# The output projection's x traffic moves to SyncE, and its first chunk starts inside the memory attention

## The reference, cut to what matters

```python
mixed = jnp.concatenate([out_a, out_b, out_m], axis=-1)   # 1024 x 2048
return x + mixed @ w_o                                    # w_o is 2048 x 2048
```

## Time and profile before

| | us |
|---|---|
| median of 3 runs | 1513.98 (1510.68 to 1514.11) |
| profiled execution, its own time | 1507.98 |
| its span in the profile | 1506.2 |
| PE busy, of the span | 1464.1 (97%) |
| DVE, ACT busy | 671.9, 469.2 |

### The profile page before, as it was taken

The page is one execution under the profiler, slowest core; times in us unless marked ns, Lnnn a source line. Parts: engine busy times, 40 slices in busy tenths (PEclk is TensorE's granted clock), DMA queues, the critical chain, the costliest instruction groups (busy, mean ns, idle before and its releaser), DMA issues.

```text
span 1506.2 us, 17987 instructions
## 1 busy us (share of the span) xinstructions
PE 1464.1 (97%) x7118; PEld 1195.7 (79%) x7118; DVE 671.9 (45%) x1055; ACT 469.2 (31%) x842; POOL 130.6 (9%) x141
## 2 busy tenths in 40 slices
PE   9999999999999999999999998889998999999997
PEld 7888888888888888887887787656777788888886
DVE  4332241442614131312226767975659654444542
ACT  4551301313131020201234456974456411111110
POOL 1010000202001000000001022100000011111110
PEclk9999999999999999999999999999999999999999
DMA  9541231121123121221444521540020233333331
GB/s 359 196 107 56 98 111 55 42 101 52 42 102 108 57 97 56 81 72 43 167 154 155 181 84 42 155 127 15 15 71 17 75 112 106 105 112 105 108 109 49
DMA packets 48812, 146.78 MB, mean 97 GB/s; under 512 B 5616, under 2 KB 9712, under 8 KB 47472
## 3 DMA queue, kind: packets, MB, share of 16 engines
q1 hardware_dynamic: 33136, 84.42, 17.8%
q0 software_dynamic: 15472, 61.51, 11.7%
q10 hardware_dynamic: 144, 0.02, 0.0%
HBM read 117.61 MB, written 28.32 MB: 97 GB/s over the span
## 4 chain that ended last, share of the span: by engine, by line
PE 90%; ACT 5%; DVE 3%; issue 1%; DMA 0%; POOL 0%; ACTq 0%; SPq 0%; DVEq 0%
PE ps L1537 26%; PE ps L1539 26%; PE ps L1538 26%; ACT a_p L805 3%; PE ps L1756 2%; PE ps L1719 2%; PE ps L1720 2%; PE ps L1737 1%; PE ps L1723 1%; PE ps L1762 1%; PE ps L1591 0%; PE ps L1590 0%; DVE w_lo L938 0%; ACT st L803 0%; PE ps L1741 0%
## 5 line engine op out<-in xcount | busy, mean ns | idle before, releaser
L938 DVE TENSOR_TENSOR w_lo<-w_raw,w_hi 128x1024 fp32r<-128x1024 f32 x87 | 106.6, 1225 | 504.0 <-ACT w_hi L608 503.6
L608 ACT ACTIVATE w_hi<-w_raw 128x1024 fp32r<-128x1024 f32 x89 | 94.2, 1059 | 593.8 <-PE ps L1539 573.9
L1537 PE MATMUL ps<-w_hi,h_hi 128*128 128x512 f32 x640 | 249.5, 390 | 1.4 <-DVE h_lo L953 1.4
L1539 PE MATMUL ps<-w_hi,h_lo 128*128 128x512 f32 x640 | 249.4, 390 | 0.0
L1538 PE MATMUL ps<-w_lo,h_hi 128*128 128x512 f32 x640 | 249.3, 390 | 0.0
L1539 PE MATMUL ps<-h_hi,w_lo 128*128 128x512 f32 x512 | 199.5, 390 | 0.0
L1537 PE MATMUL ps<-h_hi,w_hi 128*128 128x512 f32 x512 | 199.5, 390 | 0.0
L1538 PE MATMUL ps<-h_lo,w_hi 128*128 128x512 f32 x512 | 199.5, 390 | 0.0
L1538 PE MATMUL ps<-mixed_lo,z_hi 128*128 128x512 f32 x384 | 149.6, 390 | 0.0
L1537 PEld LDWEIGHTS ps<-w_hi,h_hi 128*128 128x128 f32 x640 | 120.2, 188 | 26.5 <-issue 1.6
L1539 PEld LDWEIGHTS ps<-w_hi,h_lo 128*128 128x128 f32 x640 | 120.2, 188 | 24.9
(11 more groups left out here) (270 smaller groups left out, 2090.9 us busy)
## 6 DMA issues: line engine op xcount, KB each, us to landing
w_raw<-in_w SPq DMA_DIRECT2D x89, 512.0 KB, 3.5
z<-in_w_out SPq DMA_DIRECT2D x64, 256.0 KB, 2.7
x_nat<-in_x POOLq DMA_DIRECT2D x8, 1024.0 KB, 8.6
mixed<-gate_s POOLq DMA_DIRECT2D x16, 512.0 KB, 4.9
xq<-in_xT POOLq DMA_DIRECT2D x32, 256.0 KB, 4.5
out_y<-xq POOLq DMA_DIRECT2D x32, 256.0 KB, 2.6
x_raw<-in_xT SPq DMA_DIRECT2D x7, 1024.0 KB, 18.2
gate_s<-T POOLq DMA_DIRECT2D x3, 2048.0 KB, 7.0
```

What stands on the lines that cost most here:

```text
L608: a.activation(w_hi[:, n % SPLIT, :], w_raw[:, n % RAW, :], ACT.Copy).then_inc(hi_ready, 1)
L938: v.tensor_tensor(w_lo[:, n % SPLIT, :], w_raw[:, n % RAW, :], w_hi[:, n % SPLIT, :].bitcast(F32), ALU.subtract).then_inc(lo_ready, 1)
L1537: mm(out, a_hi, b_hi, start=start, stop=False)
L1539: return mm(out, a_lo, b_hi, start=False, stop=stop)
```

## The change

- The order of the units in a visit becomes 0, 1, 4, 2, 5, 3, 6, 7 (`ORDER`, `unit(c)`), in the loads of z and on all engines; the weights are read from the same array at the other index.
- The x loads and the stores of the result go from POOL's queue to SP's, between the loads of z.
- PE does chunk 0's products P1, P5, P7, P2, P3 inside or just after the last steps of the memory attention, P4 behind the last value product, and P6 behind the last gate.
- Preparation is redistributed, in `ahead` and in the first chunks of the projection, and three buffers change place.

```diff
+ORDER = (0, 1, 4, 2, 5, 3, 6, 7)
@@ sync (SP)
-                sp.dma_start(z[c % ZRING][:, 0:4, :], io["w_out"][c]).then_inc(z_loaded[c % ZRING], 16)
+                sp.dma_start(z[c % ZRING][:, 0:4, :], io["w_out"][c // NUNIT * NUNIT + unit(c)]).then_inc(z_loaded[c % ZRING], 16)
+            def load_xq(visit):
+                for q in range(4):
+                    wait(sp, xq_moved[q], 32 * visit)
+                    sp.dma_start(xq[:, q, :], quad(io["xT"], visit, q)).then_inc(xq_moved[q], 16)
+            def store_y(visit):
+                for q in range(4):
+                    sp.wait_ge(drained, 9 * visit + 6 + q)
+                    sp.dma_start(quad(io["yT"], visit, q), xq[:, q, :]).then_inc(xq_moved[q], 16)
             for c in range(2, NOUT):
                 load_z(c)
+                if c == 2:
+                    load_xq(0)
+                if c >= NUNIT and c % NUNIT == 3:
+                    store_y(c // NUNIT - 1)
+                if c >= NUNIT and c % NUNIT == 4:
+                    load_xq(c // NUNIT)
+            store_y(NVISIT - 1)
@@ gpsimd (POOL): its loads of x and stores of the result are removed
@@ scalar (ACT)
             def ahead(c):
-                if 2 <= c <= 5:
-                    left_high(1 + (c - 2) // 2, c % 2)
-                if c == 6:
-                    z_high(0)
+                if c in (2, 3):
+                    left_high(1, c - 2)
+                if c == 5:
+                    act.wait_ge(B.pv, len(BSTEPS))
+                if c in (4, 5):
+                    z_high(c - 4)
+                if c in (6, 7):
+                    left_high(2, c - 6)
+                    plain_high(c + 2)
...
-            act.wait_ge(M.gated, TT)
+            act.wait_ge(M.pv, TT)
             for c in range(NOUT):
-                if c + 1 < NOUT:
+                if 2 <= c + 1 < NOUT:
                     z_high(c + 1)
-                if c == 0:
+                if c in (1, 3, 4):
+                    k = {1: 10, 3: 12, 4: 14}[c]
+                    plain_high(k)
+                    plain_high(k + 1)
+                if c == 2:
                     left_high(3, 0)
                     left_high(3, 1)
-                elif c < 5:
-                    for k in (2 * c + 6, 2 * c + 7):
-                        plain_high(k)
-                if u == NBLOCK:
+                if c % NUNIT == 6:
@@ vector (DVE)
             def ahead(c):
-                if c < 4:
-                    left_sums(1 + c // 2, c % 2)
-                elif c < 6:
-                    left_low(1, c - 4)
-                    if c == 5:
-                        z_make(0)
-                else:
-                    left_low(2, c - 6)
+                if c in (0, 1):
+                    left_sums(1, c)
+                if c in (2, 3):
+                    z_make(c - 2)
+                if c in (5, 6):
+                    z_low(c - 5)
+                if c in (4, 5):
+                    left_sums(2, c - 4)
+                if c in (6, 7):
+                    left_low(1, c - 6)
...
-            z_low(0)
             gate(M, TT - 1, 1, TT // 2 - 1)
-            z_make(1)
             for c in range(NOUT):
-                if c + 1 < NOUT:
+                if 2 <= c + 1 < NOUT:
                     z_low(c + 1)
-                if c == 0:
+                if c == 2:
                     left_sums(3, 0)
                     left_sums(3, 1)
-                elif c < 3:
-                    left_low(3, c - 1)
-                if 2 <= c <= 6:
-                    for k in ((8,), (9, 10), (11, 12), (13, 14), (15,))[c - 2]:
-                        plain_low(k)
-                if u == (6 if visit == 0 else 4):
+                if c in (0, 2, 4, 5):
+                    k = {0: 8, 2: 10, 4: 12, 5: 14}[c]
+                    plain_low(k)
+                    plain_low(k + 1)
+                if c in (1, 3):
+                    left_low(2 + c // 2, 0)
+                    left_low(2 + c // 2, 1)
+                if u == 6:
                     partial_sums(visit)
-                if u == (7 if visit == 0 else 5):
+                if u == 7:
                     add_sums(visit)
@@ tensor (PE), in the memory attention's step body
+                        if beside and c == n - 1:
+                            beside(1)
...
                             value(at_, c - 1, 1 - par, i if par else i - 1)
+                        if beside and c == n - 2:
+                            beside(0)
                         turn_p(at_, c, par)
@@ tensor (PE)
+            def out_begun(part):
+                if part == 0:
+                    pe.wait_ge(z_lo_made, 1)
+                    pe.wait_ge(left_lo_made, 2)
+                    pe.wait_ge(M.qT, TT)
+                    product(0, P1)
+                elif part == 1:
+                    pe.wait_ge(M.exp, TT)
+                    product(0, P5)
+                    product(0, P7)
+                else:
+                    product(0, P2)
+                    product(0, P3)
...
+            out_begun(2)
+            value(M, TT - 1, 1, TT // 2 - 1)
-            pe.wait_ge(M.gated, TT)
             for c in range(NOUT):
...
+                if c == 0:
+                    product(0, P4)
+                    pe.wait_ge(M.gated, TT)
+                    ins = product(0, P6)
```

More of the change, by code:

```diff
@@ L266, in layer @@
         left_slo = [at(f"left_slo{u}", [P, 3, HALF], F32R, left_at[u] + 14336) for u in range(NBLOCK)]
-        plain_at = [RT + 8192, RT + 12288] + [RS + 4096 * k for k in range(6)]
+        plain_at = [RT + 12288, RS, small_at + 3584, RS + 4096, RS + 8192, RS + 12288, RT, RT + 4096]
         plain_hi = [at(f"plain_hi{k}", [P, SEQ], F32R, plain_at[k]) for k in range(KT - 2 * NBLOCK)]
@@ L271, in layer @@
         z_lo = [at(f"z_lo{i}", [P, 7, P], F32R, z_at[i]) for i in range(ZRING)]
-        zh_at = (R0 + 61440, small_at + 3584)
+        zh_at = (R0 + 61440, RT + 8192)
         z_hi = [at(f"z_hi{i}", [P, 7, P], F32R, zh_at[i]) for i in range(HRING)]
[L274 to L277, removed]
+        xq = at("xq", [P, 4, HALF], F32, small_at + 7680)
+        part_a = at("part_a", [P, HALF], F32, small_at + 15872)
+        part_b = at("part_b", [P, HALF], F32, small_at + 17920)
+        assert small_at + 19968 <= nc.sbuf_usable_end
         ps = ctx.enter_context(nc.psum_tensor("ps", [P, 8, HALF], F32))
@@ L365, in blocks_to, with unit @@
         def blocks_to(c):
-            return NBLOCK * (c // NUNIT) + min(c % NUNIT, NBLOCK - 1) + 1
+            return NBLOCK * (c // NUNIT) + sum(u < NBLOCK for u in ORDER[:c % NUNIT + 1])
+        def unit(c):
+            return ORDER[c % NUNIT]
         def rotary_place(t):
@@ L462, in load_z, with quad @@
                     sp.wait_ge(M.gated, TT)
-                sp.dma_start(z[c % ZRING][:, 0:4, :], io["w_out"][c]).then_inc(z_loaded[c % ZRING], 16)
+                sp.dma_start(z[c % ZRING][:, 0:4, :], io["w_out"][c // NUNIT * NUNIT + unit(c)]).then_inc(z_loaded[c % ZRING], 16)
+            def quad(a, visit, q):
+                return a[2 * visit + q % 2, :, q // 2 * HALF:(q // 2 + 1) * HALF]
+            def load_xq(visit):
[6 more added lines that the diff above has]
+                    sp.dma_start(quad(io["yT"], visit, q), xq[:, q, :]).then_inc(xq_moved[q], 16)
             for c in range(2):
@@ L470, in _ @@
                 load_z(c)
+                if c == 2:
[5 more added lines that the diff above has]
+            store_y(NVISIT - 1)
+            for q in range(4):
+                sp.wait_ge(xq_moved[q], 32 * NVISIT)
         @block.gpsimd
@@ L573, in _ @@
                                ).then_inc(M.gates_loaded, 16)
[L575 to L590, removed]
         def gate_sigmoid(act, a, group):
@@ L879, in z_high @@
             def z_high(c):
-                n = 7 if c % NUNIT < NBLOCK else 4
+                n = 7 if unit(c) < NBLOCK else 4
                 act.wait_ge(z_made, blocks_to(c)) if n == 7 else act.wait_ge(z_loaded[c % ZRING], 16 * (c // ZRING + 1))
@@ L907, in _ @@
                 m_tiles(i)
-            act.wait_ge(M.gated, TT)
+            act.wait_ge(M.pv, TT)
             for c in range(NOUT):
-                visit, u = c // NUNIT, c % NUNIT
-                if c + 1 < NOUT:
+                visit = c // NUNIT
+                if 2 <= c + 1 < NOUT:
                     z_high(c + 1)
-                if c == 0:
+                if c in (1, 3, 4):
[3 more added lines that the diff above has]
+                if c == 2:
                     left_high(3, 0)
                     left_high(3, 1)
-                elif c < 5:
-                    for k in (2 * c + 6, 2 * c + 7):
-                        plain_high(k)
-                if u == NBLOCK:
+                if c % NUNIT == 6:
                     act.wait_ge(summed, 7 * visit + 1)
@@ L1414, in z_make @@
             def z_make(c):
-                if c % NUNIT >= NBLOCK:
+                if unit(c) >= NBLOCK:
                     return
```

(29 more changed lines are left out.)

## The result

The changed kernel takes 1500.89 us (median of 4 runs, 1498.93 to 1504.40), the kernel before 1513.58 (4 runs, 1510.68 to 1514.11): a ratio of 0.9923, 95% interval 0.9900 to 0.9945. It is 12.7 us faster. The forecast was 3.9 us and the time lies outside the stated range. Two executions of the kernel before in the later series lay far outside the rest (5271.8 and 1656.5 us); no ratio uses them.

A forecast was written before the change was run, and what follows sets the result against it. PE was taken to bound the kernel, busy 97% of the span with 9.8 us idle to win. Attention and first projection chunks gain 3.9 us, later visits and tail 0: 1513.98 - 3.9 = 1510.1 us, 8 in 10 within 1505.0 to 1514.5.

The forecast's parts named there:

- The bound and PE's idle time: Whole kernel: PE works 97% of the span; 9.8 us idle from 1140 to 1186 us, none in later visits.
- two waits under 0.8 us: PE, 1140 to 1186 us: small waits said to make the rest of the 9.8 us idle.
- the difference to the median: Whole kernel: 3.9 us taken off the 1513.98 us median, as the profiled execution was 6 us under it.
- The count through the queues: Memory attention and first projection chunks: step-by-step count through the engines' queues, gain 3.9 us.
- The waits it named: PE idle: 1.1 us before step 7's transposes, 2.4 before chunk 4, 1.5 before chunk 5.
- The rivals: Four other cases: late z 3 (18%), costly filled products (8%), no new projection waits (12%), z behind x (7%).
- No product in the attention delayed a transposition: Memory attention, rival at 8%: filled products cost what they fill, up to 2.0 us, time 1512.0.
- PE has no wait in the later visits: Later visits: PE has no idle time, so nothing to win and cost 0; a wait there would show it wrong.
- no z load landed later than 5.2 us: Visits 1 to 7, rival at 7%: z behind x lands at 8 us, loses 6.6 net, 1520.6.
- The late z 3: First projection chunks, rival at 18%: z 3 behind four x quarters lands 1.4 us late, gain 2.5, time 1511.5.
- The tail: Kernel's end: SP replacing POOL for stores counted as 0, bounds 0.3 gained to 1.9 lost; tail of 9.8 us expected.
- the whole forecast would have been 4.3 us: Tail: by the skill's first-byte figures, 0.6 against 1 us, the sum would be 4.3; not adopted.

The follow-up runs named there:

- the second trace: The kernel before, unchanged, traced again as a control: median 1512.36 us (12 runs), ratio 0.9992 to the kernel before.
- the second series: The changed kernel, unchanged, timed again beside runs of the kernel before: 1501.19 us, ratio 0.9915 (0.9901 to 0.9929).
- chunk 0 late: The changed kernel with PE beginning chunk 0 only after the last gate: 1503.47 us, ratio 0.9935 to the kernel before.

## Why the prediction was wrong

**The bound and PE's idle time: right.** 9.8 us of idle time before, and no gain in the later visits: the pace there is the same in both. (Of the "two waits under 0.8 us" that made its rest the view shows one, of 0.5; nothing hangs on it.) To take the difference to the median and not to the profiled execution was right too: the second trace takes the same 381.35 us in the stage and is 4 us longer ahead of it.

**The count through the queues: right.** 3.9 us forecast; 4.1 and 3.9 measured between the same instructions. The waits it named are there: 2.2 us before chunk 4 (2.4 forecast), 1.2 before chunk 5 (1.5) where the clock doesn't cover it, 0.9 before the transposes of step 7 (1.1), and the last wait for ACT's copy that was left. Chunk 0's early start is worth 2.3 us by the medians (2.2 by the same count), 2.6 to 3.1 by the traces. The rivals did not occur. No product in the attention delayed a transposition, PE has no wait in the later visits, and no z load landed later than 5.2 us. The late z 3 came closest: behind the four x quarters it took 5.1 us (6.6 in the rival) and landed 0.4 us before DVE's queue came to it, at 1179.86 against 1180.25 in the changed kernel's first trace.

**The tail: the step that failed.** The text took 0 for SP in place of POOL, with bounds of 0.3 gained and 1.9 lost. It measured 6.5 us gained (9.7 against 3.2 in the first two pairs). The mistake was to price only the issue and the landing. The earlier trace rows put the last store's landing at about 1497.46 + 2.3 = 1499.8, and the span ends at 1506.2: 6.4 us of the tail had no row and I took them as fixed. 5.95 of them were POOL's closing drain, and the changed kernel has POOL finished 370 us earlier. The bounds came from rows of transfers, and most of the cost was not in a transfer. What was in one, issue and landing, gained 0.56 us, beyond the bound of 0.3 too. The Trainium skill (DMA: Bandwidth & Descriptors, Specifications) gives about 0.6 us to the first byte from SyncE and about 1 us from GpSimd. The traces agree in direction: the last four stores, each alone, landed 2.00 to 2.02 us after their issue from SP and 2.27 to 2.31 from POOL. By that figure the whole forecast would have been 4.3 us, so it does not reach the drain either. (Over all stores the medians are 3.5 from SP and 2.6 from POOL, but in the visits SP issues its four 0.5 us apart and POOL 0.6 us or more, beside other transfers, so these don't compare the two alone.)

**The rest.** 3.9 and 6.5 make 10.4 us, against 12.4 to 12.7 between medians. The table gives a mean of 382.6 us for the old order and 377.4 for the new, so 1.2 us more than the chain's 3.9, with half-clock stretches that the old order meets in four of seven traces. That makes 11.6, inside the interval of the second series (10.7 to 15.0 us). What is left, about 1 us, was not pinned down. The 1.2 us is a mean over few traces, and that the idle time brings the half-clock stretches is only suggested by them: of seven traces with nearly the same idle time three have none, and no run changed the idle time alone.

## What to carry to other kernels

Price the end of a kernel to the last event of the span, and not to the last row the profile names: a gap there belongs to somebody. In this kernel the engine that issued the last stores and finished last paid its closing work in the open; look at what each engine's closing work takes, give the last stores to one that closes quickly, and let the others be done early. A count through strictly ordered queues, with start-to-start durations, was right within 0.2 us in the traces of two schedules; in the third (chunk 0 late) it was right by the medians and 0.4 to 0.9 us short by the trace. The waits that it finds are worth moving a piece of work for: without two of them the kernel was 4.1 us faster by the trace.

## What the runs showed of the hardware

- POOL's closing DRAIN took 5.95 us right behind the landing of its last stores, 6.5 where it started with the last store's issue, 5.6 behind the landing of its last x load, 5.0 to 5.2 where it started with the issue of its last gate load, and 2.36 where that load lay 370 us back. SP's took 0.01 where SP finished last, and 0.13 in the kernel before, where it didn't.
- A store of 256 KB that runs alone landed 2.0 us after its issue from SP and 2.3 from POOL (the last four stores). In the visits, where SP issues four of them 0.5 us apart, they landed 3.0 to 5.2 us after their issue.
- TensorE at the lower of its two levels (1.2 GHz) ran a 128x512 matmul every 0.43 us instead of 0.23, as in these rows of the changed kernel's first trace behind the wait before chunk 4:

```profile
1190.78 0.80 PE L1556 MATMUL ps<-plain_hi,z_hi 128*128 128x512 f32 x1 [2.17 <-DVE z_lo L1447]
1191.37 0.63 PE L1557 MATMUL ps<-mixed_lo,z_hi 128*128 128x512 f32 x1
1191.80 0.63 PE L1558 MATMUL ps<-plain_hi,z_lo 128*128 128x512 f32 x1
...
1194.20 0.39 PE L1558 MATMUL ps<-plain_hi,z_lo 128*128 128x512 f32 x1
1194.43 0.39 PE L1556 MATMUL ps<-plain_hi,z_hi 128*128 128x512 f32 x1
```
